# Up-projection biases seeded into PSUM by ScalarE instead of added by TensorE, with the experts taken in an alternating order

## The reference, cut to what matters

```python
logits = (t @ w_router + b_router).astype(jnp.float32)
top_vals, top_idx = lax.top_k(logits, TOP_K)            # 4 of 32
gate = jax.nn.softmax(top_vals, axis=-1)
def expert_block(args):                                  # 128 tokens of one expert
    xb, e = args
    h = xb @ w_up[e] + b_up[e]                           # (128, 2048); the bias is what the change moves
    g = jnp.minimum(h[:, :D_FF], SWIGLU_LIMIT)
    lin = jnp.clip(h[:, D_FF:], -SWIGLU_LIMIT, SWIGLU_LIMIT)
    act = g * jax.nn.sigmoid(SWIGLU_ALPHA * g) * (lin + 1.0)
    return act @ w_down[e] + b_down[e]
```

## Time and profile before

| | us |
|---|---|
| median of 3 runs | 2228.92 |
| lowest and highest | 2226.05, 2230.78 |
| profiled execution, its own time | 2227.35 |
| its span in the profile | 2225.6 |

### The profile page before, as it was taken

How to read it: one execution, slowest core, us unless ns; L and a number is a source line. 1 busy time by engine, 2 the same in 40 slices (tenths; PEclk the granted TensorE clock), 3 DMA queues, 4 the chain that set the end, 5 groups by cost and what they waited for, 6 DMA issues and landing times.

```text
span 2225.6 us, 33282 instructions
## 1 busy us (share of the span) xinstructions
PE 2126.1 (96%) x10402; PEld 1765.4 (79%) x10403; DVE 1610.5 (72%) x1858; ACT 1211.4 (54%) x1251; POOL 587.9 (26%) x589
## 2 busy tenths in 40 slices
PE   7999987997899999999999999999999999999996
PEld 6887987686588888888888878887888888878785
DVE  4688977447855665778698675977976887677766
ACT  4423262331545554666577564757755676565655
POOL 1001031106511111334053050513511252131404
PEclk9999999997899999999999999999999999999998
DMA  7123275512976765979699795988986898777967
GB/s 186 58 86 139 86 164 190 185 57 86 351 260 215 226 223 179 338 246 373 228 359 378 233 331 180 362 284 286 364 310 224 284 369 308 244 244 282 309 238 271
DMA packets 287303, 541.66 MB, mean 243 GB/s; under 512 B 37302, under 2 KB 53798, under 8 KB 286146
## 3 DMA queue, kind: packets, MB, share of 16 engines
q1 hardware_dynamic: 262866, 495.07, 63.9%
q0 software_dynamic: 24368, 45.72, 8.2%
HBM read 513.61 MB, written 65.13 MB: 260 GB/s over the span
## 4 chain that ended last, share of the span: by engine, by line
PE 55%; issue 6%; DVE 6%; ACT 3%; DMA 3%; ACTq 0%; DVEq 0%; POOL 0%; SPq 0%; POOLq 0%
PE ex_ps_l L2945 7%; PE ex_ps_l L2944 7%; PE ex_ps_g L2944 6%; PE ex_ps_g L2945 6%; PE ex_ps_y L2944 5%; PE ex_ps_y L2945 5%; PE ex_ps_l L2948 4%; PE ex_ps_g L2948 4%; PE ex_ps_y L2948 3%; DVE ex_w_lo L2711 3%; PE ex_ps_t L2882 2%; ACT ex_w_hi L2579 2%; DMA ex_late<-in_w_down_dram 2%; PE ex_ps_t L2892 2%; PE ex_ps_g L2954 1%
## 5 line engine op out<-in xcount | busy, mean ns | idle before, releaser
L2711 DVE TENSOR_TENSOR ex_w_lo<-ex_late,ex_w_hi 128x2048 fp32r<-128x2048 f32 x204 | 464.2, 2291 | 222.5 <-ACT ex_w_hi L2579 154.7
L2411 POOL TENSOR_TENSOR ex_passed<-keep_ident 128x1 f32<-128x1 f32 x136 | 125.7, 924 | 1102.2 <-ACT ex_y L2622 1077.9
L2579 ACT CAST ex_w_hi<-ex_late 128x2048 fp32r<-128x2048 f32 x170 | 324.5, 1909 | 115.7 <-PE ex_ps_g L2945 60.7
L2711 DVE TENSOR_TENSOR ex_w_lo<-keep_sig_o,ex_w_hi 128x2048 fp32r<-128x2048 f32 x136 | 309.6, 2288 | 100.1 <-ACT ex_w_hi L2579 100.1
L2579 ACT CAST ex_w_hi<-keep_sig_o 128x2048 fp32r<-128x2048 f32 x134 | 255.1, 1904 | 120.6 <-PE ex_ps_l L2945 37.0
L2944 PE MATMUL ex_ps_l<-ex_w_hi,ex_x_hi 128*128 128x512 f32 x784 | 308.6, 394 | 2.0 <-DVE ex_w_lo L2711 2.0
L2944 PE MATMUL ex_ps_g<-ex_w_hi,ex_x_hi 128*128 128x512 f32 x784 | 306.5, 391 | 3.8 <-DVE ex_w_lo L2711 2.1
L2945 PE MATMUL ex_ps_l<-ex_w_lo,ex_x_hi 128*128 128x512 f32 x784 | 305.5, 390 | 0.0
L2945 PE MATMUL ex_ps_g<-ex_w_lo,ex_x_hi 128*128 128x512 f32 x784 | 305.1, 389 | 0.0
L2944 PE MATMUL ex_ps_y<-ex_w_hi,ex_h_hi 128*128 128x512 f32 x544 | 217.3, 400 | 1.2 <-DVE ex_h_lo L2747 0.9
L2945 PE MATMUL ex_ps_y<-ex_w_lo,ex_h_hi 128*128 128x512 f32 x544 | 212.1, 390 | 0.0
(11 more groups left out here) (507 smaller groups left out, 4114.2 us busy)
## 6 DMA issues: line engine op xcount, KB each, us to landing
keep_sig_o<-in_w_up_dram SPq DMA_DIRECT2D x102, 1024.0 KB
ex_late<-in_w_up_dram SPq DMA_DIRECT2D x102, 1024.0 KB
ex_late<-in_w_down_dram SPq DMA_DIRECT2D x102, 1024.0 KB
keep_weights<-in_w_up_dram SPq DMA_DIRECT2D x68, 1024.0 KB
keep_sig_o<-in_w_down_dram SPq DMA_DIRECT2D x34, 1024.0 KB
st_tab<-tabs SPq DMA_DIRECT2D x8, 1408.0 KB, 12.4
keep_weights<-in_w_in_dram SPq DMA_DIRECT2D x5, 1024.0 KB, 5.5
pr_late_pieces<-in_w_in_dram SPq DMA_DIRECT2D x5, 1024.0 KB
```

What stands on the lines that cost most here:

```text
L2411: pool.tensor_tensor(passed[:, :], ident[:, 0:1], ident[:, 0:1], ALU.add).then_inc(passed_done, 1)
L2579: nc.scalar.copy(w_hi[:, j % SPLIT, :, :], raw(j)).then_inc(hi_done, 1)
L2711: v.tensor_tensor(w_lo[:, j % SPLIT, :, :], raw(j), w_hi[:, j % SPLIT, :, :].bitcast(F32), ALU.subtract).then_inc(lo_done, 1)
```

## The change

**Bias.** The one-hot products, `pick`, `choose`, `bias_hl` and its preparation are gone. ACT issues one DMA per pass that spreads the next expert's `b_up` row (8 KB) over 128 partitions into the tile `bias` (1 MB written), and copies halves of it into the PSUM banks ahead of the products, which then accumulate onto it (`start=False` for all of the up projection). The linear half gets its + 1 by the activation's bias operand, and in small pairs a per-partition factor makes the upper 64 rows of the second block zero. A single has four such copies ("seeds"), a pair eight. PE waits for them at chunks 0, 2, 4 and 6.

**Order.** The plan is now sorted by turns: expert 0 first, then of experts 1 to 30 a pair and a single in turn, and expert 31 last. The word of a turn holds the expert, its pass number and the next turn's expert. For this DVE has 20 more small instructions in `plan_with_bias`, and PE one more matmul in between (`take_turns`).

With the same experts the 34 passes become: s F s h s h s F s h s (h s) s h s F s h s h s (h s) s h s h s h s h s s. Ten singles now come right after a small pair of another expert, two after the small pair of their own, three after a full pair, and three after a single (the last pass among them).

```diff
+                def load_bias(e):
+                    act.dma_start(bias[:, :], p["b_up"][0][bass.ds(e, 1), :].to_broadcast([P, 2 * F])).then_inc(bias_in, 16)
+                def load_next_bias(n, e_next):
+                    act.wait_ge(l_seeded, n * 2 + 2)
+                    load_bias(e_next)
+                def seed_g(bank, half, above=False):
+                    scale = one_above[:, 0:1] if above else 1.0
+                    return nc.scalar.activation(bank[:, :], bias[:, half * 512:half * 512 + 512], ACT.Copy, scale=scale)
+                def seed_l(bank, half, above=False):
+                    plus = one_above[:, 0:1] if above else one[:, 0:1]
+                    scale = one_above[:, 0:1] if above else 1.0
+                    return nc.scalar.activation(bank[:, :], bias[:, F + half * 512:F + half * 512 + 512], ACT.Identity,
+                                                bias=plus, scale=scale)
...
                     if kind is not ALONE:
                         for b in range(1, blocks):
                             x_high(n, kind, blocks, b, x_turn_no(kind, b), SMALL if small else P)
+                    if blocks == 2:
+                        act.wait_ge(y_b_read, n + 1)
+                        seed_g(ps_g[1], 0, small).then_inc(g_seeded, 1)
+                    if kind is not ALONE:
                         hi(n, SPLIT - 1, True)
+                    if blocks == 2:
+                        seed_l(ps_l[0], 0)
+                        seed_l(ps_l[1], 0, small).then_inc(l_seeded, 1)
+                    else:
+                        act.wait_ge(y_b_read, n + 1)
+                        seed_l(ps_l[0], 0).then_inc(l_seeded, 1)
+                        seed_g(ps_g[1], 1).then_inc(g_seeded, 2)
+                        seed_l(ps_l[1], 1).then_inc(l_seeded, 1)
+                        if kind is AHEAD:
+                            load_next_bias(n, e_next)
                     for j in range(CHUNKS):
+                        if blocks == 2 and j == 2:
+                            act.wait_ge(glu_done, n * 10 + 3)
+                            seed_g(ps_g[0], 1)
+                            seed_g(ps_g[1], 1, small).then_inc(g_seeded, 1)
+                        if blocks == 2 and j == 4:
+                            act.wait_ge(lin_read, n * 4 + 2)
+                            seed_l(ps_l[0], 1)
+                            seed_l(ps_l[1], 1, small).then_inc(l_seeded, 1)
+                            if kind is AHEAD:
+                                load_next_bias(n, e_next)
...
+                        if kind is AHEAD and j == 10:
+                            act.wait_ge(glu_done, n * 10 + 7)
+                            seed_first(n + 1)
...
-                        if j == 9 and kind is AHEAD:
-                            choose(n + 1, e_next)
...
+                    elif j in (2, 6):
+                        pe.wait_ge(l_seeded, n * 2 + (j // 4 + 1))
...
-                        if up and part == 1:
-                            if j == 1:
-                                pe.wait_ge(bias_set, 1)
-                                pe.wait_ge(bias_zeroed, 1)
-                            col = (j // 2) % 2 * F + (j // 4) * 512
-                            mm = pe.matmul(to[:, :], pick[:, b, :], bias_hl[:, col:col + 512], start=False, stop=True)
```

## The result

The changed kernel takes **2258.4 us** (median of 4 runs, 2256.4 to 2259.0), the kernel before 2228.0 beside it: a ratio of **1.0132** (95% interval 1.0116 to 1.0148), 1.3% slower. The forecast was 2248 with a range of 2224 to 2263. The profiled execution has a span of 2256.6 us, 31.0 more than that of before; the forecast's sum was 20.7.

A forecast was written before the change was run, and what follows sets the result against it. PE, busy 96%, bounds pairs; singles last 28.6 us from chunk 4 on DVE. Pairs -27.2, singles +42.1, plan +3.3, first pass +2, last +0.5 sum to +20.7 on 2227.35: 2248 us, range 2224 to 2263.

The forecast's parts named there:

- Pairs, -27.2: In 15 pairs PE is the bound; dropping bias products saves 1.81 us each, seeds being covered by two chunks of PE time.
- The rule for singles: A single lasts 28.6 us from the start of chunk 4 on DVE, unless PE itself needs longer.
- A single after a single, 37.3: Each of the two singles following a single in the loop takes 37.3 us, where it now takes 36.1.
- rival (c): Bias load delays weights in all 19 singles, 2.8 us per pass: +53 us, 2300; chance 0.08 in full or part.
- the ring's lead: Six weight chunks of lead, refilled in pairs, keep the bias load from delaying weights with at most two singles together.
- Order, +6.5 in the 42.1: Within the singles' +42.1 us: ten late starts instead of five, at 37.4 instead of 36.1 us.
- Plan, +3.3: 20 more small DVE instructions in a stretch without DVE idle time: +3.3 us (bounds 2.5 and 5).
- First pass, +2: First pass has full DMA engines and gets 1.5 MB more, less 0.9 us of products: +2 us (bounds -0.9 and +3.2).
- Last pass, +0.5: Last pass, a single after a single without a DMA issue: +0.5 us (bounds -0.9 and +1.5).
- (a): Products were the bound and seeds hide: all 44.5 us go, 5.5 come back, 2190 us; chance 0.12.
- (b): Cheap seeds, free issue: about 1.1 us less for each of 17 singles, 2230 us; chance 0.10 (2222 to 2235).
- The forecast's comparison: Seeds priced from silu and y_out rows; faster PSUM access would mean 3 us less over 17 singles, untested by any row.

The follow-up runs named there:

- The late seeds: Changed kernel with only chunk 2's seed between ACT's chunks 3 and 4 of a single; other seeds and the load's issue come after chunks 5 and 7: ratio 1.0077.
- The small load: Changed kernel whose later bias loads bring one 8 KB row to one partition instead of 1 MB to 128; issue, waits and seeds stay: ratio 1.0101.
- the order alone: Kernel before with only the new order of passes and its plan; the bias products stay: ratio 1.0087, +19.4 us.
- late seeds and no load: Changed kernel with seeds moved later in singles and a single bias load ahead of the loop, none in it: ratio 0.9978.

## Why the prediction was right, point by point

- **Pairs, -27.2**: right. 68.1 and 57.2 against 68.0 and 57.2; the cover held, no pair has idle time.
- **The rule for singles** (28.6 us from chunk 4 on DVE): right. 40.0 against 39.8, 37.7 against 37.9, 38.4 against 38.0. The prices were near, too: seeds recorded with 0.69, 0.58 and 0.67 and 0.62 and 0.52 apart, wait and issue 0.76 of idle time. Chunk 3 starts 5.12 us after the pass's start and not 4.84, which accounts for the 0.2 above the forecast. The late seeds, which move only this work, bear it out for 0.8 to 1.8 of their 1.9 us.
- **A single after a single, 37.3**: wrong, at both places where it occurs in the loop. It takes 40.9 and 40.7 with transposes, 40.1 and 39.9 without: 5.4 us missed. I had weighed this as rival (c) and given it little, because the ring's lead would do for two singles together. The step that failed is that lead, for which the prediction had only rows of passes without the load's megabyte: the second single moves 15.5 MB (379 GB/s for 40.9 us) at a share of 1.05, where the same kind before moved 13.5 in 36.1. The small load shows it: 38.3. Part of the loss is the clock that follows PE's wait of 3.23 us (0.96 over the pass).
- **Order, +6.5 in the 42.1**: the passes right, the whole too small. Missed: the gap of 3.76 us ahead of the last pass, which makes pass 2157.2 43.9 instead of 39.8 us (4.1), where the natural order had 2.09 at that place and 2 us of it were in my base already.
- **Plan, +3.3**: +2.9, near the forecast. DVE's last `add_bias` ends 4.25 us later (570.49 against 566.24) and the expert stage starts 4.8 later, but 1.35 of this was there before the plan began: the copy of the counts starts at 556.57 against 555.22. In the 13 profiles that copy starts anywhere from 547.7 to 556.6 us, with either plan, so the 1.35 cannot be put down to the change.
- **First pass, +2**: +0.9. The sign and cause were right (the small load gives back 2.6), but the load's own share there was not known ahead. **Last pass, +0.5**: +0.2.

The misses add up: the 17 singles took 684.3 us where the forecast had 662.3 + 14 x 0.8 = 673.5, so 10.8 more; with +1.5 for the start, -1.1 for the first pass, -0.3 for the last and -0.6 in pairs that is 10.3, and 20.7 + 10.3 = 31.0, the difference of the spans. The direction rests on the mechanism forecast, the size on it and on 10 us of two others. That the time still lies within 2224 to 2263 is owed to the width of that range: none of its bounds stood for these two.

Of the rivals, (a) is refuted by the kernel without products, which gains 32 us without paying anything. (b) would have needed the cheaper prices; the issue, which it took for nearly free, is worth 14 us when it is taken away. (c) is true in part, as said.

The Trainium skill ("ScalarE: Activation LUTs", Step-by-step: what each stage is for) says that ScalarE reaches PSUM faster than SBUF. The forecast's comparison cannot test that, since a seed (SBUF to PSUM, 0.58 us) and `silu` (PSUM to SBUF, 0.60) differ in source and destination at once. A nearer pair in the changed kernel's trace, both from SBUF and 128x512, is a cast to SBUF with a mean of 620 ns (L1797) and the gate seed to PSUM with 601 ns (L2677): 3% less, which agrees in sign, though the two differ in operation and type as well.

What stays open: why PE's gap ahead of the last pass is 3.76 us after a single and about 2 after a pair (the profile shows no releaser), and why the first pass is 3.1 us longer with the order alone. Neither was tried apart. Nor is it shown how one load makes 8.3 us in the meeting of two singles with late seeds.

## What to carry to other kernels

Before work is moved off the engine that is busy for 96%, look for the stages in which it is really alone: here pairs gave back every matmul (1.8 us each), while a single paid for what was put between two chunks on ScalarE (2.6 us more there, 2.6 us more of the pass), since ScalarE, VectorE and TensorE formed one chain with next to no slack. An engine's mean idle time says nothing about such a chain. And where stretches already run at the full DMA rate, count the bytes of a broadcast as written (1 MB for 8 KB), and put edit and load only into the passes that have room for both.

## What the runs showed of the hardware

A wait of 2.1 us of PE was followed in some passes by a lower clock, in others not, with the same instructions. In the changed kernel, 3 us of the single of 788.9 and of the single of 886.9, each 9.1 us after the pass's start:

```profile
798.00:801.00 3.00, 3.00 (x9) 2.35 (x8) 0.92 (x2) 2.63 (x3) 2.03 (x6) 0.50 0.96 298
896.00:899.00 3.00, 3.00 (x14) 2.46 (x14) 0.90 (x2) 2.60 (x3) 2.03 (x6) 1.00 1.00 299
```

At 0.50 (1.2 GHz instead of 2.4) matmuls start 0.43 us apart instead of 0.227, as the 9 and 14 of the rows show. It costs nothing here, since DVE is later anyway and both passes take 40.8 us. With late seeds and no load, where chunk 4 reaches DVE earlier and PE is nearer to being last, the singles after another expert's small pair that have a low clock (0.96 over the pass) take 40.0 us and the others 39.0, the one ahead of the last pass aside. After the gap of 3.7 to 3.8 us it came in all seven profiles that have this gap: in the changed kernel the clock is 0.71 over the first 4.9 us of the last pass, where before it was 1.00.

The second surprise was the price of a DMA issue on a busy engine: recorded with 0.35 us, it cost 0.5 to 0.9 us of every single, with its wait and its register work. Issued while a long cast was still running (896.11, in the cast of 895.10), it left no gap on ScalarE, and then its transfer ran beside the weights of chunk 10, which landed later.
